# Freeing half a weight slot at a time in a three-block layer chain kernel

## The reference, cut to what matters

```python
# block 1: h = x
h = h + stick_breaking_attention(rms_norm(h, norm_mix), w_in, w_out)      # 16 heads of 64
h = h + swiglu(rms_norm(h, norm_ffn), ffn_w_in, ffn_w_out)                # 2816 hidden
h = h + sigmoid(rms_norm(h, norm_ple) @ ple_w_gate) * (p @ ple_w_proj)
h = rms_norm(h, final_norm)
# block 2: gated convolution of width 31 and retention (4 heads of 256), side by side
proj = (rms_norm(h) * (1 + scale) + shift) @ w_in
...
h = h + gate * (concat([y_conv, y_ret]) @ w_out)
h = rms_norm(h, final_g)
# block 3: an S5 branch and an SSD branch, side by side, then a gate
u_s5, z_s5, z_ssd, xBC, dt_raw = split(rms_norm(h) @ w_in)
...
h = h + concat([y_s5, y_ssd]) @ w_out
h = h + (p @ w_ple_proj) * sigmoid(rms_norm(h) @ w_ple_gate)
return rms_norm(h, final_norm_w)
```

## Time and profile before

| | |
|---|---|
| median of 3 runs | 3850.46 us |
| lowest and highest | 3846.21, 3852.64 us |
| the profiled execution | 3852.6 us, of which its span is 3850.4 us |
| mean granted clock of TensorE | 0.978 |
| busy share of the span | PE 95%, PE weight loads 76%, DVE 54%, POOL 30%, ACT 24% |
| DMA | 260 MB, mean 68 GB/s |

### The profile page before, as it was taken

The page is one execution under the profiler, slowest core; times in us unless marked ns, Lnnn a source line. Parts: engine busy times, 40 slices in busy tenths (PEclk is TensorE's granted clock), DMA queues, the critical chain, the costliest instruction groups (busy, mean ns, idle before and its releaser), DMA issues.

```text
span 3850.4 us, 46324 instructions
## 1 busy us (share of the span) xinstructions
PE 3664.4 (95%) x18230; PEld 2909.7 (76%) x18230; DVE 2096.2 (54%) x2828; ACT 940.7 (24%) x1672; POOL 1138.9 (30%) x1069
## 2 busy tenths in 40 slices
PE   6999999899999999999999999879999999999998
PEld 5677776688888877788886777558878877787776
DVE  5455546633333346799934453464715497663564
ACT  3434344400000004211101101140322112552132
POOL 2121312233333333333331232123223233014433
PEclk9999999999999999999999999989999999999999
DMA  2000100121212121122221121211174324432111
GB/s 94 18 28 23 34 23 23 50 71 60 65 60 71 55 70 39 39 99 87 78 70 61 39 77 50 82 61 60 66 155 106 81 77 115 148 101 80 66 55 66
DMA packets 139240, 260.20 MB, mean 68 GB/s; under 512 B 45632, under 2 KB 87616, under 8 KB 136000
## 3 DMA queue, kind: packets, MB, share of 16 engines
q1 hardware_dynamic: 72208, 156.26, 14.0%
q10 hardware_dynamic: 66864, 101.62, 7.7%
HBM read 209.35 MB, written 46.14 MB: 66 GB/s over the span
## 4 chain that ended last, share of the span: by engine, by line
PE 86%; DVE 9%; ACT 2%; DMA 1%; issue 1%; POOL 1%; SPq 0%; ACTq 0%; DVEq 0%; POOLq 0%
PE bank L602 23%; PE bank L603 23%; PE bank L604 23%; PE bank L842 2%; PE bank L1020 2%; PE bank L879 2%; PE bank L862 2%; PE bank L1009 1%; DVE fb L2144 1%; DMA raw<-in_wstream 1%; PE bank L724 1%; PE bank L1181 1%; PE bank L1164 1%; DVE ab L2147 1%; DVE h L2536 1%
## 5 line engine op out<-in xcount | busy, mean ns | idle before, releaser
L602 PE MATMUL bank<-xh,wh 128*128 128x512 f32 x3024 | 1194.6, 395 | 32.5 <-POOL wl L571 12.6
L603 PE MATMUL bank<-xl,wh 128*128 128x512 f32 x3024 | 1184.4, 392 | 0.0
L604 PE MATMUL bank<-xh,wl 128*128 128x512 f32 x3024 | 1183.6, 391 | 0.0
L569 POOL CAST wh<-raw 128x512 fp32r<-128x512 f32 x528 | 382.7, 725 | 2508.6 <-PE bank L604 2458.8
L571 POOL TENSOR_TENSOR wl<-raw,wh 128x512 fp32r<-128x512 f32 x528 | 755.3, 1430 | 42.3
L602 PEld LDWEIGHTS bank<-xh,wh 128*128 128x128 f32 x3024 | 569.9, 188 | 177.2 <-issue 31.6
L604 PEld LDWEIGHTS bank<-xh,wl 128*128 128x128 f32 x3024 | 570.0, 188 | 123.2 <-issue 1.4
L603 PEld LDWEIGHTS bank<-xl,wh 128*128 128x128 f32 x3024 | 570.4, 189 | 118.2 <-issue 1.6
L2313 DVE SCALAR_TENSOR_TENSOR bank<-apad,cols,bank 128x512 f32<-128x512 f32 x406 | 267.9, 752 | 0.0
L2049 DVE TENSOR_TENSOR h<-bank,h 128x512 f32<-128x512 f32 x240 | 165.5, 691 | 157.4 <-PE bank L604 157.0
L2144 DVE TENSOR_TENSOR_SCAN fb<-fb 128x256 f32<-128x256 f32 (+7 forms) x128 | 182.3, 1465 | 68.7 <-ACT ab L1386 68.7
(11 more groups left out here) (333 smaller groups left out, 5024.9 us busy)
## 6 DMA issues: line engine op xcount, KB each, us to landing
raw<-in_wstream SPq DMA_DIRECT2D x264, 512.0 KB, 3.5
spills<-spill ACTq DMA_DIRECT2D x38, 512.0 KB, 2.7
rawm<-in_mod_w ACTq DMA_DIRECT2D x12, 1024.0 KB, 4.9
gate_spill<-gates ACTq DMA_DIRECT2D x16, 512.0 KB, 2.6
tabs<-in_rope ACTq DMA_DIRECT2D x4, 2048.0 KB, 8.3
f<-spills SPq DMA_DIRECT2D x8, 1024.0 KB, 6.0
h<-in_x ACTq DMA_DIRECT2D x4, 1024.0 KB, 11.7
tabs<-gate_spill ACTq DMA_DIRECT2D x4, 1024.0 KB, 4.9
```

The lines of the kernel that those rows point to most:

```text
L569: nc.gpsimd.tensor_copy(wh[:, slot, k], raw[:, slot, k]).then_inc(S("panel_high"), 1)
L602: nc.tensor.matmul(o, lh, rh, start=start, stop=False)
L603: nc.tensor.matmul(o, lh, rl, start=False, stop=False)
L604: return nc.tensor.matmul(o, ll, rh, start=False, stop=stop)
```

## The change

- PE gets a second counter, `unit_half`: each unit signals it once its first four slabs (or, for the units of an output panel, the first of its two) are used. It is one more increment on a matmul that is there anyway; no instruction is added on PE.
- POOL waits for each half on its own: for the first half of a panel until `unit_half` has reached the number of the slot's last user, less `PANEL_BACK` (0 for plain and value panels, 3 for output panels, 7 for the one-slab panels of attention), and for the second half until `unit_done` has reached it, as before.
- A value unit runs over the halves first: slabs 0 to 3 for both token groups, then slabs 4 to 7 for both. Both groups accumulate in the same bank at once; only the very first matmul of the unit starts the bank.
- For two value pairs (attention's `v0` and retention's `v0`) POOL splits the first halves of both panels before the second halves (`SPLIT_TOGETHER`). The counts that PE and SP wait for follow this order (`split_count`, `stream_around`).

```diff
+    for part in halves:
         k = slice(part * SLABS, (part + 1) * SLABS)
+        if freed is not None and part == 0:
+            pool.wait_ge(S("unit_half"), freed.value(-back))
+        if freed is not None and part == 1:
+            pool.wait_ge(S("unit_done"), freed.value())
         nc.gpsimd.tensor_copy(wh[:, slot, k], raw[:, slot, k]).then_inc(S("panel_high"), 1)
...
-                if freed is not None:
-                    pool.wait_ge(S("unit_done"), freed.value())
...
+            def v_unit(unit, panel, u):
+                bank_free(unit)
+                for half in range(2):
+                    split_done(panel + 1, half)
+                    for q in range(2):
+                        t = slice((2 * u + q) * P, (2 * u + q + 1) * P)
+                        for k in range(half * SLABS, (half + 1) * SLABS):
+                            mm = mm3(banks[u % 2][:, q * 256:(q + 1) * 256], xh[:, k, t], xl[:, k, t],
+                                     wh[:, :, k, :], wl[:, :, k, :], q == 0 and k == 0, k == KT - 1, shared=True)
+                    mm.then_inc(S("unit_done" if half else "unit_half"), 1)
...
         mm = mm3(banks[th][:, :], wh[:, slot, slab, :], wl[:, slot, slab, :],
                  rh[:, t], rl[:, t], n == 0, n == len(slabs) - 1)
+        if n == len(slabs) // 2 - 1:
+            mm.then_inc(S("unit_half"), 1)
...
+SPLIT_TOGETHER = [PANEL0["attn"] + ATTN_PANEL["v", 0], PANEL0["ret"] + RET_PANEL["v", 0]]
+def split_count(panel, part):
+    if panel in SPLIT_TOGETHER:
+        return 2 * panel + 2 * part + 1
+    if panel - 1 in SPLIT_TOGETHER:
+        return 2 * panel + 2 * part
+    return 2 * panel + part + 1
...
+    if PANEL0[name] + m in SPLIT_TOGETHER:
+        order[m:m + 2] = [(m, [0]), (m + 1, [0])]
+        order[m + 2:m + 2] = [(m, [1]), (m + 1, [1])]
```

More of the change, by code:

```diff
@@ L94, in pair_tile @@
     return (u % 2, u // 2) if paired else (u // 2, u % 2)
+OUT_BACK, HALF_BACK = 3, 7
 def attention_order():
-    unit_of, panel_of, freed, fills, n_panels = {}, {}, [], {}, 0
+    unit_of, panel_of, freed, back, fills, n_panels = {}, {}, [], [], {}, 0
     def project(name):
@@ L111, in project @@
         freed.extend([first + n] if dp == 1 else [first + n] * 2 if kind == "v" else [first + 8, first + 16])
+        back.extend({"out": [OUT_BACK] * 2, "half": [HALF_BACK]}.get(kind, [0] * dp))
         return keys
@@ L127, in attention_order @@
     end = project("half7")
-    return unit_of, panel_of, freed, start, fills, end
-ATTN_UNIT, ATTN_PANEL, ATTN_FREED, ATTN_START, ATTN_FILLS, ATTN_END = attention_order()
+    return unit_of, panel_of, freed, back, start, fills, end
+ATTN_UNIT, ATTN_PANEL, ATTN_FREED, ATTN_BACK, ATTN_START, ATTN_FILLS, ATTN_END = attention_order()
 RET_ORDER = [("v", 0)] + [x for hd in range(RET_HEADS) for x in
@@ L162 @@
     PANEL_UNITS[_name] = [2, 4]
+PANEL_BACK = {name: [0] * len(freed) for name, freed in PANEL_UNITS.items()}
+PANEL_BACK["attn"] = ATTN_BACK
+PANEL_BACK["ffn"] = [OUT_BACK if n % 6 >= 4 else 0 for n in range(12)]
+for _name in ("ffn_last", "side1", "side3"):
+    PANEL_BACK[_name] = [OUT_BACK] * 2
+PANEL_BACK["ret"] = [b for kind, _ in RET_ORDER for b in {"v": [0] * 2, "qk": [0] * 4, "out": [OUT_BACK] * 2}[kind]]
+for _name in ("pw", "glu"):
+    PANEL_BACK[_name] = [b for kind, _ in TURN_ORDER for b in {"in": [0] * 2, "out": [OUT_BACK] * 2}[kind]]
 COLS, _c = {}, 0
@@ L507, in stream_one, with stream_around @@
             def stream_one(q):
-                sp.wait_ge(S("panel_split"), 2 * (q - 1))
+                sp.wait_ge(S("panel_split"), split_count(q - 2, 1))
                 sp.dma_start(raw[:, q % 2].rearrange("p k n -> p (k n)"), wstream[q]).then_inc(
                     S(f"panel_in{q % 2}"), 16)
+            def stream_around(first, last):
+                for p in SPLIT_TOGETHER:
+                    if p + 4 <= last:
+                        if p + 2 > first:
+                            stream(first, p + 2)
+                        for q in range(p + 2, p + 4):
+                            stream_one(q)
+                        first = p + 4
+                stream(first, last)
             if "s5_z" not in run:
-                stream(2, n_panels)
+                stream_around(2, n_panels)
             else:
                 q0 = PANEL0["s5_u"] + 4
-                stream(2, q0)
+                stream_around(2, q0)
                 sp.wait_ge(S("norm_low"), SPLIT0["second_final"] + 2 * KT)
@@ L551, in _, with split @@
             nc.gpsimd.memset(eps[:, :], EPS).then_inc(S("eps"), 1)
-            def split(panel, freed, gains=None):
+            def split(panel, freed, back, gains=None, halves=range(2)):
                 slot = panel.b % 2
@@ L574, in turn @@
             def turn(name, i, before):
-                for m in range(PANELS[name]):
-                    split(panels(name, i) + m, before[m] if m < 2 else units(name, i) + freed_after(name, i, m - 2),
-                          "ssd_norm_w_3" if name == "ssd_out" else None)
+                order = [(m, range(2)) for m in range(PANELS[name])]
+                if i is None:
+                    for m in range(PANELS[name]):
+                        if PANEL0[name] + m in SPLIT_TOGETHER:
+                            order[m:m + 2] = [(m, [0]), (m + 1, [0])]
+                            order[m + 2:m + 2] = [(m, [1]), (m + 1, [1])]
+                for m, halves in order:
+                    freed, back = before[m] if m < 2 else (units(name, i) + freed_after(name, i, m - 2),
+                                                           PANEL_BACK[name][m - 2])
+                    split(panels(name, i) + m, freed, back, "ssd_norm_w_3" if name == "ssd_out" else None, halves)
             def freed_after(name, i, m):
@@ L611, in split_done @@
             def split_done(panel, part):
-                pe.wait_ge(S("panel_split"), panel.double(part + 1))
+                pe.wait_ge(S("panel_split"), split_count(panel.b, part) if panel.i is None else panel.double(part + 1))
             def tile(unit, slot, slabs, rhs, between=None, split=None, panel=None):
@@ L801, in attn_project @@
                                  xl[:, k, t], k == 0, k == KT - 1)
+                        if k == SLABS - 1:
+                            mm.then_inc(S("unit_half"), 1)
                     mm.then_inc(S("unit_done"), 1)
                 elif kind == "v":
[L804 to L812 removed]
+                    v_unit(unit, panel, u)
                 else:
@@ L977, in ret_v @@
                 for u in (2 * half, 2 * half + 1):
[L978 to L986 removed]
+                    v_unit(unit + u, panel, u)
             def retention(n):
```

48 lines of the change are left out of this document (19 added, 29 removed).

## The result

The changed kernel takes 3813.3 us (median of 4 runs, 3807.12 to 3814.83), against 3851.55 us for the kernel before in the same series (3846.21 to 3853.01). The ratio is 0.9897 with a 95% interval of 0.9885 to 0.9909: 38 us faster. I had forecast 3830 with a range of 3822 to 3840. The direction was right, and the size was short by 17 us.

A forecast was written before the change was run, and what follows sets the result against it. The prediction took PE, busy for 95% of the span, as the bound. Gaps of 16.0 us plus 4.6 for the clock made 20.6 us, taking the median from 3850.5 to 3830, range 3822 to 3840.

The forecast's parts named there:

- Part 1, the gaps: Where PE waits for POOL's splits: halves freed earlier remove or shorten these gaps, 16.0 us gained in all.
- attention's v0: First value panel behind attention's interleaved q and k panels: 4.04 us idle, loss falls to 0, 4.2 us gained.
- retention's v0: Retention's first value panel: 2.39 us lost before, about 0.6 us of new wait for second halves, 1.8 us gained.
- the qk panel: Panel behind retention's v0: 2.23 us idle, both halves split in time, 2.3 us gained.
- each of three output panels: Behind v1, v2 and v3 of retention: 2.19 us idle and 2.35 lost each, all of it gained, 7.0 us together.
- The second halves: Rival: PE waits again at second halves, splittable only at the unit's end; 7.7 us gained, 3843; chance 0.05.
- All the signs that I had named for being right: POOL waits 18.9 to about 8.5 us, three 2.19 us gaps gone, full clock behind both v0, L709 gap 7.5 or more.
- Part 1, its first sentence on plain panels: Plain panels: nothing to gain, as a panel lasts PE 10.9 us and the other slot was split long before.
- Part 2, dt: dt panel: its 4.04 us gap shrinks to about 2.1, but PE then waits longer for DVE; 0 gained.
- Collisions: DVE's stretch from 3054.8 to the S5 output: POOL's shifted splits hit other taps, gaining 1.6 us or losing some 3.
- Part 3, the clock: Three low-clock stretches behind gaps that go: 4.6 us gained if PE doesn't stop there, bounds 0 and 5.1.
- Part 4, what is added: 890 added increments on PE's matmuls, no instruction: cost taken as 0, bounds 0 and 4.5 us.

The follow-up runs named there:

- e2: Changed kernel, but the panels where PE waited for POOL wait for the whole slot again and no first halves are split together: 3828.15 us, 0.9944 of the kernel before.
- e3: Changed kernel, but attention's panels 4 to 31 wait for the end of their slot's last unit again: 3820.77 us, 0.9927 of the kernel before.
- e9: e3 with POOL's splits in attention held until DVE finished that step's scans, except panels 9, 17 and 25: 3815.99 us, 0.9910 of the kernel before.
- e4: The changed kernel itself, run again unmodified in the series of the follow-up runs: 3812.15 us, 0.9901 of the kernel before.
- e6: Kernel before, with 17, 9 and 9 dummy matmuls filling the gaps at attention's v0, retention's v0 and the first qk panel: 3852.15 us, ratio 1.0003.
- e5: e3 with POOL's splits of twenty attention panels held until DVE finished that step's scans: 3845.18 us, 0.9982 of the kernel before.

## Why the prediction was off

**Part 1, the gaps: right.** The distances from start to start, between the same matmuls of both kernels, shrank by 4.2 at attention's v0 (forecast 4.2), 1.9 at retention's v0 (1.8: the start of v0 gained 2.4, and the new wait of 0.41 before its second halves costs 0.5; I had made that wait 0.6), 2.4 at the qk panel (2.3), 2.35 at each of three output panels (2.35) and 0.38 at each first pair (0.22, since I had left out the 0.16 us by which my own price exceeds the idle time). That is 16.7 us against 16.0. The second halves didn't become a new wait at attention's v0, at qk or at the outputs. All the signs that I had named for being right came true (7.7 us of waits for POOL, full clock behind both v0, 8.04 us before L772). They spoke of the gaps alone, so they couldn't tell that more than the gaps had moved.

**Part 1, its first sentence on plain panels: wrong, and the main error.** "In plain panels there is nothing to gain" was derived from PE's waits for POOL. It is true that PE never waits for POOL there. But in these stages POOL's step lengthens DVE's instructions under it, and in attention and retention PE waits for DVE. e2, which changes just these panels, is 22.5 us faster than the kernel before. In idle time it is 7.3 us, and 13.9 us are PE's busy time. The sum of what matmuls lose at half speed, counted as above, fell by 14 us (56 to 42), 11 of them in attention. That the waits shrink because the splits leave the scans is shown by e3 and e9; that the clock stays up because the waits shrink is only seen to go together, and e9, with two half-speed stretches in attention, didn't test it.

**Part 2, dt: right. Collisions: right in kind, applied to one stretch only.** The dt gap halved to 2.08 us and the wait before L772 grew by 2.5 to 8.04, so all of it was absorbed. (the earlier trace rows stands for two waits of DVE; that view has a third of 0.2 us, which changes nothing.) The row of a tap that takes 5.49 us instead of 3.93 showed the cost of a collision, and I used it only where DVE runs without a pause. "The gaps before attention's output units are DVE's: 0" is where it can be seen best, though it is small (0.8 us over 13 waits). The gap was DVE's, and it fell from 1.98 to 1.49 us, since the `ab` step ahead of it on DVE was hit less (2.19 us before, 1.78 after, for the same two instructions). A gap that DVE ends is no reason for zero as long as the change moves what slows DVE.

**Part 3, the clock: mis-sized.** I counted the three stretches behind gaps that go, 4.6 us. They went. But the sum of what the matmuls lose at half speed went from 56 us to 36 in e4 (33 in the profiled execution of the changed kernel), so by 20 to 23 us. The upper bound of 5.1 was no bound at all, because it considered only three places. The scores' part of attention alone (100 to 700 us) has 11.3 us of it, none behind a gap that POOL ends.

**Part 4, what is added: right.** 890 increments in the middle of accumulations cost nothing that is visible: matmuls of 512 columns still start 0.23 us apart over them. 827 of those that got an increment can be compared with themselves in the kernel before, outside gaps and low clock; from their start to the next one passes the same time within 0.1 ns on average. The Trainium skill (TensorE: Matmul & The Clock Gate, "The cost: per-tile semaphore tail") had spoken for about 23 us more, and no run here shows it.

Put together, for e4 against the kernel before: 40.0 us of span. 20.0 of it are idle time. In the waits of PE that make it up, 15.3 us are gaps that I had counted and 5.6 waits for DVE and ACT, dt and L772 together take back 0.6, and the waits for late loads another 0.6. The other 20.0 are busy time, and the sum of the losses at half speed fell by as much. Against my 20.6 the error is some 15 us of clock and some 4 of idle time. In attention, e3 and e9 show the collisions as a cause of the waits. For the stages behind it (e2 gains 11 us there) the same rows are there, as those of retention above, but no experiment separates them. Which gap draws the low clock in one execution stays open: in e3 a wait of 1.16 us at 302.95 drew none.

## What to carry to other kernels

List the bound engine's waits for every engine, not only for the one that the change touches, and ask of each: does the touched engine's work lie on top of what the wait is for? A step of POOL that nobody waits for can still be on the path through the DVE instruction that it slows. When many short gaps go, don't price the clock by the stretches behind the long ones: take the whole half-speed time of the profile as what is at stake, and give the range that width (here half of 168 us at the very most, and 20 to 23 in fact). Not all of it need show up in the time: e6 lost 18 us of half-speed time and gained nothing.

## What the runs showed of the hardware

- A subtraction of 128x512 on POOL takes 1.27 us alone and 3.17 under a scan of DVE, and two scans of 128x1024 take 5.50 us instead of 4.47. The Trainium skill (SBUF — State Buffer, "SBUF: two separate sides") says that a DVE instruction with two SBUF inputs and a GpSimd instruction that reads SBUF exclude each other for a whole instruction. The trace agrees. In the kernel before the first of two scans (304.52 us) takes 2.29 us, as it does undisturbed. The subtraction that starts inside it at 304.71 ends at 307.88, which is 1.07 us after that scan's end. The second scan then takes 3.29 us instead of 2.27.
- The clock falls behind short gaps as well: at 313 us behind waits of 1.16 and 0.48 us, and at half speed eight matmuls of 128 columns took 1.93 us instead of 1.06. The Trainium skill (TensorE: Matmul & The Clock Gate, "A second HAM failure mode: psum-queue depth-cycling") tells of a kernel in which frequent short idle times make the clock oscillate. The trace agrees in that short waits, of 1.16 to 2.1 us, stand ahead of every half-speed stretch of the scores' part of attention but those of e5. Filling three gaps with matmuls took the low clock away from there, and the kernel was no faster (1.0003, 0.9994 to 1.0012).
- A matmul can carry an increment in the middle of an accumulation, and two groups can accumulate in one bank by turns, at no measurable cost: 0.23 us from start to start.
